# Hybrid pool / conv / attention block: turning x with VectorE's 32x32 transposes, its squares and scaling in 16 pieces on ScalarE

## What is computed

```python
D_MODEL, SEQ, DEPTH = 1024, 4096, 1
h = rms_norm(x, ln_g)                         # x * rsqrt(mean(x*x) + eps) * g, per token
proj = jnp.einsum('bsd,de->bse', h, w_in)     # 1024 -> 2560 columns
(u_pool, g_pool, c_a, c_b, g_conv, q, k, v, g_attn) = split_columns(proj)
y_pool = pool_mixer(u_pool, ...)              # windows 2/4/8/16
y_conv = conv_module(c_a, c_b, ...)           # GLU, 31 taps, LayerNorm, SiLU, pointwise
y_attn = sliding_window_attention(q, k, v, attn_sinks)   # 8 heads, window 128
y = concat([y_pool*silu(g_pool), y_conv*silu(g_conv), y_attn*silu(g_attn)])
x = x + einsum('bse,ed->bsd', y, w_out)
return rms_norm(x, final_g)
```

## Time and profile before

| | |
|---|---|
| median of 3 runs | 1440.12 us (1439.05 to 1440.19) |
| profiled execution, its own time | 1439.26 us |
| its span in the profile | 1437.5 us |
| PE busy | 1414.5 us, 98% |
| DVE busy | 1145.6 us, 80% |
| ACT busy | 512.6 us, 36% |
| POOL busy | 386.5 us, 27% |
| share of PE in the chain that ended last | 90% |
| granted TensorE clock | 9 tenths or more in all 40 slices |

### The profile page before, as it was taken

One profiled execution on the slowest core, in us unless ns is written; L12 is line 12 of the kernel. 1 busy time (PEld: TensorE's weight loads), 2 busy tenths in 40 slices (PEclk: granted clock), 3 DMA queues, 4 the chain that ended last, 5 costly groups with the idle time before them and its releaser, 6 DMA issues.

```text
span 1437.5 us, 20200 instructions
## 1 busy us (share of the span) xinstructions
PE 1414.5 (98%) x7024; PEld 1160.5 (81%) x7024; DVE 1145.6 (80%) x2313; ACT 512.6 (36%) x1253; POOL 386.5 (27%) x627
## 2 busy tenths in 40 slices
PE   6999999999999999999999999999999999999998
PEld 5878787887878787878888888888888888888886
DVE  5676757575766757577989998989899988988886
ACT  5544444445445444342112121221122243333332
POOL 4414233322324242120011010110100255555552
PEclk9999999999999999999999999999999999999999
DMA  7326070616143240817033032230327666555531
GB/s 252 129 70 253 11 279 10 255 44 232 61 166 126 79 170 10 312 34 229 1 132 122 40 132 74 87 131 15 132 88 283 259 211 199 172 160 164 160 119 73
DMA packets 79102, 196.82 MB, mean 137 GB/s; under 512 B 14400, under 2 KB 41408, under 8 KB 71360
## 3 DMA queue, kind: packets, MB, share of 16 engines
q1 hardware_dynamic: 64480, 181.40, 34.3%
q10 hardware_dynamic: 14560, 14.68, 3.8%
HBM read 114.27 MB, written 81.79 MB: 136 GB/s over the span
## 4 chain that ended last, share of the span: by engine, by line
PE 90%; DVE 7%; ACT 1%; issue 1%; DMA 1%; POOL 0%; SPq 0%; POOLq 0%; DVEq 0%; ACTq 0%
PE wide L252 13%; PE wide L254 13%; PE wide L253 12%; PE pair L252 12%; PE pair L253 12%; PE pair L254 12%; PE pair L966 3%; DVE m_tail L1723 3%; PE wide L996 2%; PE wide L997 2%; PE turn L953 2%; PE turn L254 2%; PE turn L253 2%; PE turn L252 2%; PE turn L230 1%; DVE x_first L1820 1%
## 5 line engine op out<-in xcount | busy, mean ns | idle before, releaser
L1723 DVE SCALAR_TENSOR_TENSOR m_tail<-m_tail,m_taps 128x512 f32<-128x512 f32 x480 | 338.3, 751 | 4.6
L252 PE MATMUL pair<-xT,w_hi 128*128 128x512 f32 x632 | 255.0, 403 | 5.9 <-DVE xT L245 4.2
L253 PE MATMUL pair<-xT,w_lo 128*128 128x512 f32 x632 | 247.4, 391 | 0.0
L254 PE MATMUL pair<-xT,w_hi 128*128 128x512 f32 x632 | 247.1, 391 | 0.0
L107 POOL TENSOR_TENSOR pool_carrier<-pool_carrier 128x1 f32<-128x1 f32 x83 | 25.7, 310 | 613.6 <-DVE m_meanvar L1732 398.3
L1476 POOL TENSOR_TENSOR operand_sums<-m_y 128x512 f32<-128x512 f32 x75 | 102.0, 1360 | 167.8 <-PE wide L254 116.7
L252 PEld LDWEIGHTS pair<-xT,w_hi 128*128 128x128 f32 x632 | 119.2, 189 | 32.3 <-DVE a_q L864 4.8
L254 PEld LDWEIGHTS pair<-xT,w_hi 128*128 128x128 f32 x632 | 118.9, 188 | 25.6
L253 PEld LDWEIGHTS pair<-xT,w_lo 128*128 128x128 f32 x632 | 119.4, 189 | 20.6
L252 PE MATMUL wide<-xT,w_hi 128*128 128x512 f32 x328 | 128.4, 392 | 0.0
L254 PE MATMUL wide<-xT,w_hi 128*128 128x512 f32 x328 | 127.7, 389 | 0.0
(11 more groups left out here) (240 smaller groups left out, 2926.3 us busy)
## 6 DMA issues: line engine op xcount, KB each, us to landing
xT_scratch<-xT SPq DMA_DIRECT2D x16, 2048.0 KB, 15.7
xs<-in_x_dram SPq DMA_DIRECT2D x32, 512.0 KB, 6.4
x_first<-xT_scratch SPq DMA_DIRECT2D x16, 1024.0 KB, 7.6
xT<-xT_scratch SPq DMA_DIRECT2D x16, 1024.0 KB, 9.1
combo_scratch<-stage SPq DMA_DIRECT2D x28, 512.0 KB, 3.2
m_y<-y_scratch ACTq DMA_DIRECT2D x14, 1024.0 KB, 6.6
y_scratch<-y_out SPq DMA_DIRECT2D x8, 1024.0 KB, 5.9
y_scratch<-y_out SPq DMA_DIRECT2D x16, 512.0 KB, 2.9
```

Of the source, the lines that this page charges most:

```text
L252: nc.tensor.matmul(out, w_hi, x_hi, start=first, stop=False)
L253: nc.tensor.matmul(out, w_lo, x_hi, start=False, stop=False)
L254: return nc.tensor.matmul(out, w_hi, x_lo, start=False, stop=last)
L1723: nc.vector.scalar_tensor_tensor(out=conv[:, i, :], in0=h[:, i, j:j + TB], scalar=taps[:, i, j:j + 1], in1=conv[:, i, :], op0=ALU.mult, op ...
```

## The change

x of the blocks 1 to 7 is no longer turned by TensorE. VectorE can transpose each 32x32 square within 32 partitions. So that this gives channels on partitions, x is loaded with the squares already at their places: partition 32b+s holds token s of each of 16 groups of 32 tokens (a = 0 to 15), and of it the 256 channels 256b to 256b+255. After the squares are turned, partition p holds the channels 8p to 8p+7, channel 8p+k as channel tile k. The weights w_in and the gain are loaded in this order as well. The source of a channel tile then lies in `xs` with a step of 8 elements, as do the transposes' input and output.

Since the channels of a token now lie on four partitions, its sum of squares comes from 16 pieces of 256 columns on ScalarE and a small matmul with a fold matrix on TensorE; VectorE makes the mean, GpSimd the power over 16 columns, and ScalarE scales the 16 pieces. Block 0 keeps the old path, with TensorE's transposes reading xs in steps of 8.

```diff
     def load(self, sp, n):
-        need(sp, self.turned, KT * n)
+        if n == 0:
...
+        if n == 1:
+            sp.wait_ge(self.turned, KT)
+        else:
+            sp.wait_ge(self.lo_done, KT * n)
+        width = D // SUB
+        for b in range(SUB):
+            sp.dma_start(self.groups[b * self.SQUARE:(b + 1) * self.SQUARE],
+                         self.x[0, n * TB:(n + 1) * TB, b * width:(b + 1) * width].rearrange("(a s) c -> s a c", s=self.SQUARE)
+                         ).then_inc(self.loaded[b], 16)
...
+    def square(self, act, n):
+        width = D // SUB
+        for b in range(SUB):
+            act.wait_ge(self.loaded[b], 16 * n + 16)
+        for a in range(self.GROUPS):
+            act.wait_ge(self.squared, self.squares_before(n) + max(a - SUB + 1, 0))
+            self.nc.scalar.activation(self.squares[:, a % SUB * width:(a % SUB + 1) * width], self.groups[:, a, :], ACT.Square,
+                                      accum_out=self.sumsq[:, a:a + 1]).then_inc(self.squared, 1)
...
+    def fold_sums(self, pe, n):
+
+        need(pe, self.squared, SUB + self.GROUPS * n)
+        self.nc.tensor.matmul(self.turn[0][:, 0:self.GROUPS], self.fold[:], self.sumsq[:], start=True,
+                              stop=True).then_inc(self.rstd_steps, 1)
+
+    def mean(self, dve, n):
+
+        dve.wait_ge(self.rstd_steps, self.chain(n, 1))
+        self.nc.vector.tensor_scalar(self.meansq[:], self.turn[0][:, 0:self.GROUPS], 1.0 / D, EPS, ALU.mult,
+                                     ALU.add).then_inc(self.rstd_steps, 1)
+
+    def root(self, pool, n, carrier):
+
+        carrier.pool_wait(pool, self.rstd_steps, self.chain(n, 2))
+        self.nc.gpsimd.tensor_tensor(self.rstd[:], self.meansq[:], self.power[:], ALU.pow).then_inc(self.rstd_steps, 1)
+
+    def scale(self, act, n, half):
+
+        act.wait_ge(self.rstd_steps, self.chain(n, 3))
+        for a in range(half * self.GROUPS // 2, (half + 1) * self.GROUPS // 2):
+            last = self.nc.scalar.activation(self.groups[:, a, :], self.groups[:, a, :], ACT.Copy, scale=self.rstd[:, a:a + 1])
+        if half:
+            last.then_inc(self.rstd_steps, 1)
+
+    def turn_squares(self, dve, n, parts):
+
+        dve.wait_ge(self.rstd_steps, self.chain(n, 4))
+        for part in parts:
+            view = self.squares_in[:, part * SUB:(part + 1) * SUB]
+            self.nc.vector.transpose(view, view).then_inc(self.turned, 1)
```

More of the change, by code:

```diff
@@ L173, in square, with use, chain @@
[L173 to L178, removed]
+        self.spent = sem("xT_spent")
+    def use(self, turn, squares, ident, ident_ready):
+        self.turn, self.squares, self.ident, self.ident_ready = turn, squares, ident, ident_ready
+    def chain(self, n, link):
+        return 2 * SUB + self.CHAIN * (n - 1) + link
@@ L730, in body @@
             first, final = isinstance(n, int) and n == 0, isinstance(n, int) and n == NB - 1
-            for kk in range(KT):
-                st.split_hi(act, n, kk)
+            g3_done = proj_full, filled(n - 1, slot("g3"))
+            for kk in range(0 if first else PIECE, KT):
+                st.split_hi(act, n, kk, g3_done)
                 if first and kk == 3:
@@ L753, in body @@
                 w.split_hi(act, CHUNK_Q + 1)
+            elif not final:
+                st.square(act, n + 1)
             q_hi(n, 1)
@@ L765, in body @@
                 w.split_hi(act, CHUNK_G + 1)
+            elif not final:
+                st.scale(act, n + 1, 0)
             if final:
@@ L772, in body @@
                 w.split_hi(act, CHUNK_CA)
-            act.wait_ge(st.squared, SUB * NB if final else SUB * (n + 2))
+            if not final:
+                for half in range(0 if first else 1, 2):
+                    st.scale(act, n + 1, half)
+            act.wait_ge(st.squared, st.squares_before(NB if final else n + 2))
             copy_out(n, slot("v"), vT)
@@ L781, in body @@
                 exps(n, j, 0)
+                if j == SUB - 1 and not final:
+                    for kk in range(PIECE):
+                        st.split_hi(act, n + 1, kk)
                 if j:
@@ L891, in body @@
             first, final = isinstance(n, int) and n == 0, isinstance(n, int) and n == NB - 1
-            for kk in range(KT):
+            if not first:
+                output(n - 1, 2, (n - 1, slot("o2")))
+            for kk in range(0 if first else PIECE, KT):
                 st.split_lo(dve, n, kk)
-                if not first and kk == 1:
-                    output(n - 1, 2, (n - 1, slot("o2")))
             if first:
@@ L912, in body @@
                 make_combos(n, (t,) if t < 3 else (3, 4))
+                if t == (3 if first else 2) and not final:
+                    st.mean(dve, n + 1)
                 if final and t >= 2:
@@ L920, in body @@
                         pT_copy(4 * n + j - 1, 1)
+                turning_x = j == 0 and not final
+                if turning_x:
+                    st.turn_squares(dve, n + 1, range(2))
                 invert(4 * n + j, j % 2, 0)
+                if turning_x:
+                    st.turn_squares(dve, n + 1, range(2, SUB))
+                lo_pieces = range(PIECE if j == SUB - 1 and not final else 0)
+                for kk in lo_pieces[:PIECE // 2]:
+                    st.split_lo(dve, n + 1, kk)
                 if j:
                     gate_make(n, j)
+                for kk in lo_pieces[PIECE // 2:]:
+                    st.split_lo(dve, n + 1, kk)
                 invert(4 * n + j, j % 2, 1)
@@ L984, in project @@
                               st.lo[:, kk, :], kk == 0, kk == KT - 1)
+                if name == "g3" and kk == PIECE - 1:
+                    last.then_inc(st.spent, 1)
                 if between and kk < KT - 1:
@@ L1012, in body @@
                 st.first_transposes(pe)
-            else:
-                for kk in range(TURNS):
-                    if kk == 2:
-                        need(pe, score_taken, 8 * n)
-                    st.transpose(pe, n, kk)
-            project(n, "k", lambda kk: st.transpose(pe, n, kk + TURNS) if kk + TURNS < KT else None)
-            if first:
+                project(n, "k", lambda kk: st.transpose(pe, kk + TURNS) if kk + TURNS < KT else None)
                 project(n, "q0")
             else:
+                project(n, "k")
                 project(n, "q0", turning(4 * n - 1, 3))
                 attend(pe, 4 * n - 1, 3, (n, slot("o3")))
+            final = isinstance(n, int) and n == NB - 1
             for name in ("q1", "q2", "q3", "v"):
                 project(n, name)
+                if name == ("v" if first else "q2") and not final:
+                    pe.wait_ge(st.ident_ready, 8)
+                    st.fold_sums(pe, n + 1)
             for name in ("q2", "q3"):
```

119 lines of the change are left out of this document (68 added, 51 removed).

## The result

The changed kernel takes 1531.85 us (median of 4 runs, 1530.36 to 1535.01), the kernel before 1439.87 (1439.05 to 1440.19): ratio 1.0643, interval 1.0624 to 1.0661. The forecast was 1448 in 1434 to 1490. The sign is right and the size is not: +92.0 us instead of +8.7.

A forecast was written before the change was run, and what follows sets the result against it. TensorE, busy for 98%, bounds the kernel; the 29.6 us removed are given back in waits. Block 0 +8.0, blocks 1 to 6 +3.9, block 7 -3.2: +8.7 on 1439.26, forecast 1448 us, range 1434 to 1490.

The forecast's parts named there:

- Removed from TensorE: Start of blocks 1 to 7: transposes and a 0.32 us wait go, 4.23 us a block, 29.6 us in all.
- The price of the copies and transposes: Hi and lo copies stay at 0.6 and 0.67 us back to back; a 1024-column VectorE transpose takes 1.17 us.
- Rival 1: Steps of 8 elements cost double in hi and lo copies and transposes: +56 us, 1504; chance 0.27.
- Squares, scaling, power, fold: New x work: 0.45 us a square, 3.2 us for eight scaling pieces, 2.9 us the power, 0.15 us the fold matmul.
- Rival 2: GpSimd's power over 16 columns costs 1.02 us, as over 4: 1435 us, faster; chance 0.19.
- rival 3: Waits balance: scaling at 2.6 us a half with a power of 2.9 gives +4 us, of 2 about 1440; chance 0.10.
- The scores' and v's wait: Block 4: TensorE waits 1.8 us at the first scores, ScalarE being held by the power, and 1.6 us for v.
- The loads of x: Issued after the last lo copy, landing 6.4 us after issue; up to 8 us hide.
- Block 0: 1.4 us wait for q2's bank, 6.4 more for v, probabilities 0.2 late: +8.0 us; strided weight loads left at nothing.
- Projection k: Block 4's start: TensorE waits 0.85 us for lo 4; k ends at 6.5 instead of 9.67 us, 3.2 ahead.
- Probabilities: Block 4: VectorE's transposes delay the probabilities, and TensorE waits 0.85 us for the second group.

The follow-up runs named there:

- E1: The changed kernel with channels reordered so that transposes and hi and lo copies use runs of 32 neighbouring elements instead of steps of 8: 1482.65 us, ratio 1.0298.
- E2: The changed kernel with runs of 32 for the VectorE transposes only, channels left in the wrong order: 1499.33 us.
- E3: The changed kernel with runs of 32 for the hi and lo copies only, channels left in the wrong order: 1507.48 us.
- E10: E1 with squares, mean, scaling and transposes reordered in the engines' queues, and block 0's new work behind its projections: 1442.06 us, ratio 1.0022.
- E4: Single operations without the kernel: GpSimd's product takes 0.35 us alone, 0.81 to 1.09 us beside VectorE operations with two inputs in SBUF.
- E7: The changed kernel with VectorE making g3's gate before the first two lo copies and not after: 1543.83 us.
- E12: E10 with block 1's first load of the output weights issued on SyncE ahead of the load of the next x: 1438.32 us, ratio 0.9996.
- E5: E1 with GpSimd's power over 4 of the 16 columns, so that most tokens get another token's scale: 1468.63 us.

## Why the prediction was wrong

**Removed from TensorE.** Right: 4.2 us a block less to do, and where nothing else was added, in block 7, E1 gives back 2.96 us (76.02 instead of 78.98; forecast 3.2). In the change itself TensorE's busy time rose all the same, by 12.3 us.

**The price of the copies and transposes: the step that failed most.** The prediction wrote "the hi and lo copies stay at 0.6 and 0.67 back to back, as now" and took 1.17 for a transpose. Measured back to back: 1.21 (four in 4.83), 1.13 (four in 4.52) and 2.17 (two in 4.34). The rows used had no step, and the bound was known. Rival 1 had this mechanism, near these prices (lo 1.16, hi 0.96, transpose 2.29), and 56 us for it; E1 measures 49.2, E2 and E3 56.9. It stood at 0.27 and should have led: what the prediction had on steps spoke for it, and no row spoke against it. It alone would still have given 1504 and missed, by 28 us.

**Squares, scaling, power, fold.** Right: 0.40 a square (forecast 0.45), 3.31 us a half of the scaling (3.2), the power 2.91 to 2.93 in blocks 1 to 6 (2.9). In block 0 it took 3.96, beside a VectorE operation with both inputs in SBUF; in E10, with none beside it, 2.93. That fits E4's collision; no run isolates it:

```profile
61.55 3.96 POOL L257 TENSOR_TENSOR a_rstd<-a_meansq,a_power 128x16 f32<-128x16 f32 x1 [31.77 <-DVE a_meansq L251]
...
61.50 1.23 DVE L887 TENSOR_TENSOR a_bias<-a_bias,a_gate 128x1024 f32<-128x1024 f32 x1
```

Rival 2, the short power, fell. So did rival 3, with its pieces of 2.6 us a half.

**The scores' and v's wait.** The first stood in the forecast with 1.8 us and is 2.3 in E1 and 2.4 in the change, from the cause named: ScalarE stands for the power with q3 ready behind it. The second, forecast at 1.6 us in block 4, is missing there: the scores take 1.5 us longer at the lower clock, and v is ready when TensorE comes. In blocks 1 and 3 it is 1.56 us.

**The loads of x.** Wrong: "up to 8 us hide". The page has a median of 8.3 us to landing instead of 6.4, and in block 4 the loads are issued at 395.21 and ScalarE can square at 408.26, 13.1 us later; it stands for them 2.26 us. In block 0 the wait is 5.42 us, and it makes up the larger part of v's wait of 5.83, forecast at 1.4. ScalarE's rows (the change, block 0, block 4):

```profile
44.53 0.42 ACT L221 ACTIVATE a_tanh<-xs 128x256 f32<-128x256 f32 x1 [5.42 <-DMA xs<-in_x_dram]
...
408.26 0.42 ACT L221 ACTIVATE a_tanh<-xs 128x256 f32<-128x256 f32 x1 [2.26 <-DMA xs<-in_x_dram]
...
425.04 3.31 ACT L263 ACTIVATE xs<-xs,a_rstd 128x256 f32<-128x256 f32 x8 [4.10 <-POOL a_rstd L257]
```

**Block 0.** The wait at v's transposition was 7.39 us (forecast 6.4), but the block loses 16.2 instead of 8.0: 4.4 by the late x, 1.0 by this longer wait (the power's 1.05), and the rest for the most part in slower matmuls behind the first wait. Projection k began 0.9 us earlier (14.70 instead of 15.61), and by the last matmul ahead of the wait for q2's bank TensorE had lost that again (46.90, 46.87). Whether it was by weight loads in steps of 8, which the forecast left at nothing, no run shows.

**Projection k.** Half right. The wait for lo was named; that k's first matmul needs the bank of g3 was not, though the diff and the earlier trace rows held it: 1.54 us in block 4, 10.9 us in all. E7 shows that in the kernel with steps of 8 making the gate first does not win it back; in E12 8.5 us of it remain.

**Probabilities.** The wait was forecast at 0.85 a block. It is 3.0 a block with steps of 8 (21.2 in 7), and nothing with runs of 32: a size, not a mechanism.

**What was not in the sum at all.** SyncE: the load of x now waits for the last lo copy, and block 1's first load of w_out stands behind it. It is issued at 121.44 instead of 100.25; counted from projection k's first matmul (111.91 and 93.60) that is 9.5 instead of 6.7 us, and VectorE can add 13.7 us after the issue instead of 9.7. TensorE pays 3.3 us for `y_out`, and E12 takes them back (3.7 us). The granted clock: 0.019 of 1528.6 is some 29 us of clock not granted, against 1.4 before; part of them fell in waits, so it is no term to be added. What the slower matmuls are worth the busy times show, since the change, E1, E10 and E12 all have 6814 instructions on TensorE: 1426.8, 1412.8, 1399.9 and 1398.8 us. Of the 93.9 us between the pages of the change and of E12, 28.0 are busy time and 65.9 idle. The first matmul behind each wait is in it too, at 0.50 us instead of 0.39. As an example, the 16 scores behind the wait in block 4 take 3.4 us (430.42 to 433.78) instead of 1.9.

**Together.** 92.0 = 49.2 (steps, E1) + 40.6 (order, E1 to E10) + 3.7 (SyncE, E12) - 1.5 (what is left of the gain in E12). By the pages (42.4 us between the profiled executions of E1 and E10) 12.9 of the order's share are busy time and 29.5 idle. Which share is the late x and which the power was not separated: E5 prices the power's last 1.9 us at 14.0, and both work through the same wait. The 49.2 contain E1's 3.5 us for the late first weights, so the steps themselves cost more. That E12 doesn't keep the 29.6 us removed has these known parts: 8.5 for g3's bank, 3.3 at the start for the weights (5.3 instead of 2.0), 1.8 for probabilities and 1.2 for the fold. They are about half of it; the rest stays open, and with it why blocks 2 to 4 take 78 us and blocks 5 to 7 under 77.

## What to carry to other kernels

Before work is moved to another engine, write its access steps beside the row that prices it: a row with neighbouring elements does not price one with steps of 16 bytes or more, here by a factor of 1.5 to 1.8. A long wait of TensorE also costs the slower matmuls behind it, so compare busy times as well as waits. Work taken from the bounding engine had also covered hand-overs of banks, loads and constants behind it, so list what each of them was waiting for while the removed work ran. And where a new chain crosses four engines, put its pieces where each engine already stood idle: that was worth as much here as the access steps.

## What the runs showed of the chip

- VectorE's transposes and lo copies and ScalarE's copies of 4-byte elements are as fast at a step of 2 as at 1, within 4% (1202 and 1209 ns; 745 and 740; 734 and 708), and at a step of 4 as slow as at 8 (1940 and 1964; 1117 and 1132; 1183 and 1194).
- GpSimd's power costs 0.15 to 0.16 us for each further column, up to 16; its 128x128 product takes 0.35 us, and 0.81 to 1.09 beside VectorE copies with both inputs in SBUF, one product for each copy.
- Behind a wait of 2.4 us, and an earlier one of 0.9 for q, TensorE's granted clock was 0.57 in the next 4 us and its scores 0.21 us apart instead of 0.12, so that a short wait cost more than its length.
